# A transformer's four layers on one core: matmuls of constants put into TensorE's waits, and other banks for an MLP's first chunk

## The reference

```python
# first block, per layer; h_lat is (256, 1024), h_ctx is (256, 1024)
a_lat = modulate(rms_norm(h_lat, norm1_w[layer]), ml[0], ml[1])
o_lat, o_ctx = even_mixer(...)      # layer 0: latent attention and gated linear attention
o_lat, o_ctx = odd_mixer(...)       # layer 1: gated delta rule, 8 heads
h_lat = h_lat + ml[2] * o_lat
h_lat = h_lat + ml[5] * sq_relu_mlp(modulate(rms_norm(h_lat, norm2_w[layer]), ml[3], ml[4]), w1, w2)
# second block, per layer
h = rms_norm_2(x, mix_norm_pre[l]) * (1.0 + sc_m) + sh_m
y = hybrid_mixer(h, ...)            # top-k attention and a chunked mLSTM
x = x + g_m * rms_norm_2(y, mix_norm_post[l])
h = rms_norm_2(x, ffn_norm_pre[l]) * (1.0 + sc_f) + sh_f
y = swiglu(h, w_gate_up[l], w_down[l])
x = x + g_f * rms_norm_2(y, ffn_norm_post[l])
```

## Time and profile before

| | us |
|---|---|
| median of 3 executions | 2164.08 (2161.91 to 2165.92) |
| the profiled execution | 2163.82 |
| its span, first to last instruction | 2161.9 |
| TensorE busy in it | 2004.4 (93%) |
| VectorE busy | 1521.2 (70%) |
| ScalarE busy | 907.6 (42%) |
| mean granted clock of TensorE | 0.959 |

### The profile page before, as it was taken

One profiled execution on the slowest core, in us unless ns is written; L12 is line 12 of the kernel. 1 busy time (PEld: TensorE's weight loads), 2 busy tenths in 40 slices (PEclk: granted clock), 3 DMA queues, 4 the chain that ended last, 5 costly groups with the idle time before them and its releaser, 6 DMA issues. The chain is left out here.

```text
span 2161.9 us, 39923 instructions
## 1 busy us (share of the span) xinstructions
PE 2004.4 (93%) x16706; PEld 1788.0 (83%) x16706; DVE 1521.2 (70%) x2353; ACT 907.6 (42%) x1355; POOL 142.3 (7%) x231
## 2 busy tenths in 40 slices
PE   6998988999999889899999999799899979999997
PEld 5786765788888678798888999789789979988997
DVE  6866557798777668765647787689776667966454
ACT  2435453222222244423225444456544345554443
POOL 0100000001010001201210000000000000000000
PEclk7999989999999989999999999799999999999999
DMA  8542013356453176200004777343358744323552
GB/s 326 203 145 78 2 59 136 136 176 213 161 200 145 58 255 211 104 4 3 3 3 156 250 269 272 127 165 126 136 189 285 270 152 157 136 99 120 192 177 95
DMA packets 59132, 323.92 MB, mean 150 GB/s; under 512 B 6384, under 2 KB 7536, under 8 KB 32624
## 3 DMA queue, kind: packets, MB, share of 16 engines
q1 hardware_dynamic: 33360, 228.97, 29.7%
q0 software_dynamic: 25344, 92.29, 12.0%
q10 hardware_dynamic: 288, 0.66, 0.1%
HBM read 320.84 MB, written 1.05 MB: 149 GB/s over the span
## 5 line engine op out<-in xcount | busy, mean ns | idle before, releaser
L370 DVE TENSOR_TENSOR w_low<-raw,w_high 128x1024 fp32r<-128x1024 f32 (+1 forms) x408 | 473.4, 1202 | 196.9 <-ACT w_high L362 196.7
L362 ACT ACTIVATE w_high<-raw 128x1024 fp32r<-128x1024 f32 (+1 forms) x408 | 402.6, 1034 | 363.0 <-PE banks L407 352.3
L548 DVE SCALAR_TENSOR_TENSOR mod_rows<-mod_rows,silu_condition 128x1024 f32<-128x1024 f32 x176 | 212.9, 1221 | 9.0 <-DMA mod_rows<-rows_dram 6.3
L405 PE MATMUL banks<-ffn_a_l,w_high 128*128 128x256 f32 x704 | 201.1, 286 | 8.5 <-DVE ffn_a_l L712 6.5
L406 PE MATMUL banks<-ffn_a_h,w_high 128*128 128x256 f32 x704 | 199.3, 283 | 0.0
L407 PE MATMUL banks<-ffn_a_h,w_low 128*128 128x256 f32 x704 | 199.1, 283 | 0.0
L534 POOL DMA_DIRECT2D mod_rows<-rows_dram x176 | 93.2, 530 | 1329.7 <-DVE mod_rows L548 1108.6
L405 PE MATMUL banks<-mlp_hidden_l,w_high 128*128 128x512 f32 (+1 forms) x512 | 174.7, 341 | 3.9 <-DVE mlp_hidden_l L1102 3.0
L407 PE MATMUL banks<-mlp_hidden_h,w_low 128*128 128x512 f32 (+1 forms) x512 | 174.5, 341 | 0.0
L406 PE MATMUL banks<-mlp_hidden_h,w_high 128*128 128x512 f32 (+1 forms) x512 | 174.4, 341 | 0.0
L405 PE MATMUL banks<-mix_l,w_high 128*128 128x256 f32 (+1 forms) x448 | 134.4, 300 | 14.0 <-DVE mix_l L759 12.9
(11 more groups left out here) (617 smaller groups left out, 4983.3 us busy)
## 6 DMA issues: line engine op xcount, KB each, us to landing
raw<-panels_dram SPq DMA_DIRECT2D x204, 1024.0 KB, 4.8
mod_rows<-rows_dram POOLq DMA_DIRECT2D x176, 512.0 KB, 5.1
mod_0a_rows<-rows_dram SPq DMA_DIRECT2D x8, 1024.0 KB, 19.3
x_features<-x_features_dram SPq DMA_DIRECT2D x1, 2048.0 KB, 11.2
constants<-small_dram SPq DMA_DIRECT2D x1, 1672.5 KB, 6.7
silu_condition<-conditions_dram SPq DMA_DIRECT2D x2, 512.0 KB, 12.4
out_dram<-x_features SPq DMA_DIRECT2D x4, 256.0 KB, 2.1
constants<-small_dram SPq DMA_DIRECT2D x1, 736.5 KB, 5.1
```

What stands on the lines that cost most here:

```text
L362: self.nc.scalar.activation(self.wh[:, m % 2, cols], self.raw[:, slot, cols], ACT.Copy).then_inc(self.w_high, 1)
L370: self.nc.vector.tensor_tensor(self.wl[:, m % 2, cols], self.raw[:, slot, cols], self.wh[:, m % 2, cols].bitcast(F32), ALU.subtract).then_ ...
L405: self.nc.tensor.matmul(out, sh(k), ml(k), start=(opens and k == 0), stop=False)
L548: nc.vector.scalar_tensor_tensor(row if v == nv - 1 else self.scratch[:], row, 1.0, self.cond[v][:], ALU.mult, ALU.mult, accum_out=mod[:, ...
```

## The change

Two new methods issue float32 matmuls of the constant `ones` matrix with the first 512 columns of the constants, into a bank that is free, and nobody reads the result: `keep_busy` inside a TensorE function, and `busy_before` as a function of its own. `rstd` gets a parameter `busy = (first, last, bank)`: so many ahead of the sums of squares, and so many behind them. Calls stand ahead of `even_in`, `odd_in` and `mix_in`, in the attention ahead of turns 2, 8 and 30 and ahead of the last values, in the odd mixer ahead of the first keys and in the heads' norm, at the hybrid mixer's end, in the norms, and ahead of layer 1's MLP openers. `open_sums` uses all 128 rows instead of one. In layer 0's MLP the chunks from the second on take banks 2 and 3, and the second chunk's up products no longer wait for `h_ready`.

```diff
--- before.py
+++ after.py
@@ -559,7 +559,7 @@
     def rstd(self, tmp, name, src, src_ready, groups, n, dim, matrix, bank=0, squares=None,
-             meanwhile=None, r=None, between=None, fold=0, squared=None):
+             meanwhile=None, r=None, between=None, fold=0, squared=None, busy=None):
@@ -608,8 +608,11 @@
                 act.wait_ge(root_ready, 1)
                 nc.scalar.activation(r[:], root[:], ACT.Exp, scale=-0.5).then_inc(ready, 1)
+        busy_first, busy_last, busy_bank = busy or (0, 0, 0)
+
         @self.block.tensor
         def _(pe):
+            self.keep_busy(pe, busy_first, busy_bank)
             for i, blocks in enumerate(groups):
                 if fold:
                     blocks = [0] + blocks[fold:]
@@ -625,6 +628,7 @@
                     last = nc.tensor.matmul(sums[:, i, :], matrix, squares[:, b, :],
                                             start=(b == blocks[0]), stop=(b == blocks[-1]))
             last.then_inc(summed, 1)
+            self.keep_busy(pe, busy_last, busy_bank)
         @self.block.vector
         def _(dve):
@@ -635,10 +639,10 @@
                 nc.vector.reciprocal(r[:], root[:]).then_inc(ready, 1)
         return r, squares, [(ready, 1)]
-    def next_norm(self, scope, name, n, ready, split=False, squares=None):
+    def next_norm(self, scope, name, n, ready, split=False, squares=None, busy=None):
         return self.rstd(scope, name, self.xT[:, :, 0:n], ready, [list(range(KD))], n, D, self.c("ones"), 1, squares,
-                         r=self.next_rstd[:, :, 0:n],
+                         r=self.next_rstd[:, :, 0:n], busy=busy,
                          between=(lambda act: self.split_upto("act", act, self.m)) if split else None,
                          meanwhile=(lambda dve, _: self.split_upto("dve", dve, self.m)) if split else None)
@@ -663,7 +667,7 @@
         return [(ready, nb)]
     def norm_modulate(self, name, weight, mod, nv, shift, scale, n, high, low, ready, bank=0, work=None,
-                      scaled_x=None, split_first=2):
+                      scaled_x=None, split_first=2, busy=None):
         nc = self.nc
@@ -693,7 +697,7 @@
                     last.then_inc(scaled, 1)
             r, _, r_ready = self.rstd(tmp, name, x, ready, [list(range(KD))], n, D, self.c("ones"), bank, work,
-                                      meanwhile=scale_x)
+                                      meanwhile=scale_x, busy=busy)
             @self.block.vector
             def _(dve):
@@ -936,9 +940,18 @@
     def open_sums(self, pe, banks):
-        zero, any_rows = self.c("causal")[0:1, TL:TL + P], self.cst[0:1, 0:512]
+        zero, any_rows = self.c("causal")[:, TL:TL + P], self.cst[:, 0:512]
         for b in banks:
             self.nc.tensor.matmul(self.ps[:, b, :], zero, any_rows, start=True, stop=False)
+
+    def keep_busy(self, pe, count, bank):
+
+
+        for _ in range(count):
+            self.nc.tensor.matmul(self.ps[:, bank, :], self.c("ones"), self.cst[:, 0:512], start=True, stop=True)
+
+    def busy_before(self, count, bank):
+        self.block.tensor(lambda pe: self.keep_busy(pe, count, bank))
     def open_sums_first(self, banks=(5, 6, 7)):
         self.block.tensor(lambda pe: self.open_sums(pe, banks))
@@ -975,7 +988,7 @@
         ps = self.ps
         scaled_ready, bias_ready = (self.sem(f"{name}_{s}") for s in ("scaled", "shift_product_ready"))
         bias = self.sb(f"{name}_shift_product", [P, 2, 1], ctx=tmp)
-        first_bank = 2 if deferred is not None else 0
+        first_bank = 0 if gated else 2
         up_banks = lambda cs: slice(0, 2) if cs == 0 else slice(first_bank, first_bank + 2)
         def pe_up_deferred(pe, cs, q=None):
@@ -1028,12 +1041,12 @@
             for u in range(ups):
                 self.wait_split(pe, m_of["up", cs, u], q)
                 m = m_of["up", cs, u]
-                if u == 0 and cs >= 1:
+                if u == 0 and cs >= (1 if gated else 2):
                     pe.wait_ge(h_ready, c)
                 for b in range(2):
                     if cs == 0 and u == 0 and b == 0:
                         self.operand_wait = lambda k: pe.wait_ge(a_ready[0][0], k + 1)
-                    last = self.product3(ps[:, 2 * u + b, 0:n],
+                    last = self.product3(ps[:, 2 * u + b if gated else up_banks(cs).start + b, 0:n],
                                          lambda k: self.wh[:, m % 2, k * PC + b * P:k * PC + (b + 1) * P],
                                          lambda k: self.wl[:, m % 2, k * PC + b * P:k * PC + (b + 1) * P],
                                          lambda k: high[:, k, 0:n], lambda k: low[:, k, 0:n], KD)
@@ -1075,7 +1088,7 @@
             if cs >= 1:
                 act.wait_ge(h_ready, c)
             act.wait_ge(up_done, c * ups + 1)
-            nc.scalar.activation(act_buf[:], ps[:, 0:2, 0:n], ACT.Silu if gated else ACT.Relu).then_inc(r_ready, 1)
+            nc.scalar.activation(act_buf[:], ps[:, up_banks(cs), 0:n], ACT.Silu if gated else ACT.Relu).then_inc(r_ready, 1)
         def act_high(act, cs, q=None):
             c = cs if q is None else q * per + cs
@@ -1093,7 +1106,7 @@
             if gated:
                 ins = nc.vector.tensor_tensor(hid[:], act_buf[:], ps[:, 2:4, 0:n], ALU.mult)
             else:
-                ins = nc.vector.scalar_tensor_tensor(hid[:], ps[:, 0:2, 0:n], 0.0, act_buf[:], ALU.max, ALU.mult)
+                ins = nc.vector.scalar_tensor_tensor(hid[:], ps[:, up_banks(cs), 0:n], 0.0, act_buf[:], ALU.max, ALU.mult)
             ins.then_inc(h_ready, 1)
         def dve_low(dve, cs, q=None):
@@ -1601,6 +1614,7 @@
             nc.vector.tensor_tensor(flat(cq_l[:]), flat(pa[:, 0:3, :]), flat(cq_h[:]).bitcast(F32),
                                     ALU.subtract).then_inc(cq_split, 1)
+    pr.busy_before(4, 6)
     pr.linear("even_in", 7, 2, 14, pr.features(high, low, N, KD, tall_offset), pr.copy_out(target), a_ready,
               beside=beside_in, rising=True, info=in_info)
@@ -1748,10 +1762,13 @@
         scores(2)
         for n in range(T):
             if n + 1 < T:
+                pr.keep_busy(pe, {2: 4, 8: 1, 30: 3}.get(n + 1, 0), 2)
                 turn(n + 1)
             if n + 3 < T:
                 scores(n + 3)
             gla_step(n)
+            if n + 1 == T:
+                pr.keep_busy(pe, 2, 2)
             values(n)
         for n, i in enumerate((0, 2, 1, 3)):
             pe.wait_ge(a_scaled, n + 1)
@@ -2142,6 +2160,9 @@
                 nc.tensor.matmul(ps[:, b, :], c("block64"), kT[:, b, :], start=True, stop=True).then_inc(k_summed, 1)
         def turn_keys(h):
+            if h == 0:
+                pe.wait_ge(logs, 3)
+                pr.keep_busy(pe, 3, 3)
             pe.wait_ge(normed, h + 1)
             for b in (2 * h, 2 * h + 1):
                 for i in range(4):
@@ -2653,6 +2674,8 @@
     def _(pe):
         for d in range(2):
             for h in range(2):
+                if d and not h:
+                    pr.keep_busy(pe, 2, 2 * order[1])
                 pe.wait_ge(sq_ready, 2 * d + h + 1)
                 nc.tensor.matmul(ps[:, 2 * order[d] + h, :], c("ones"),
                                  sq[:, order[d], 4 * h:4 * h + 4, :].rearrange("p h n -> p (h n)"),
@@ -2842,6 +2865,7 @@
             eng.wait_ge(cq_high, 1)
             nc.vector.tensor_tensor(cq_l[:], cq_sq, cq_h[:].bitcast(F32), ALU.subtract).then_inc(cq_split, 1)
+    pr.busy_before(3, 7)
     pr.linear("mix_in", 4, 2, 8, pr.features(high, low, N, KD, tall_offset), block_out(0), a_ready,
               engines=who[:8], rising=True, beside=beside_first, info=a_info, first_out=conv_first(0))
     sm_t = work[0:32, 0, :]
@@ -3195,6 +3219,8 @@
                                            hm[:, i, b * P:(b + 1) * P], c("ident"))
             last.then_inc(m_turned, 1)
         for i in range(2):
+            if i:
+                pr.keep_busy(pe, 2, 1)
             pe.wait_ge(o_scaled, i + 1)
             for b in range(4):
                 last = nc.tensor.transpose(ps[:, (4, 5)[b // 2], (b % 2) * N + i * P:(b % 2) * N + (i + 1) * P],
@@ -3325,10 +3351,11 @@
                 high = pr.sb("mlp0_a_h", [P, KD, n], F32R, ctx=t)
                 low = pr.sb("mlp0_a_l", [P, KD, n], F32R, ctx=t)
                 a_ready = pr.norm_modulate("norm2_0", norm("norm2", 0), mod, nv, 24, 32, n, high, low,
-                                           lambda k: [(ready[0][0], k + 1)], bank=0, scaled_x=y)
+                                           lambda k: [(ready[0][0], k + 1)], bank=0, scaled_x=y,
+                                           busy=(2, 7, 1))
                 y, y_ready = pr.feed_forward("mlp0", D_FF // 256, False, n, high, low, a_ready, y, [], beside)
                 added = pr.add_feed_forward("mlp0", y, y_ready + outs[0], mod, 40, nv, n)
-                pr.next_norm(t, "norm1_1", n, lambda k: [(added[0][0], k + 1)], split=True)
```

(16 more changed lines are left out.)

## The result

| | us |
|---|---|
| median of the kernel before, 4 executions | 2163.49 (2161.91 to 2165.92) |
| median of the changed kernel, 4 executions | 2151.7 (2148.91 to 2156.08) |
| ratio | 0.9946, 95% interval 0.9933 to 0.9959 |
| the profiled execution of the changed kernel | 2156.08, the longest of its four; span 2154.3 |

The change makes the kernel 11.8 us faster (9 to 14.5 by the interval). I had forecast 16.6 us. The sign and the main mechanism were right; the size was 40% too large (two later measurements give 12.6 and 13.3 us, and at 13.3 it is a quarter too large).

The account below looks back on a forecast made before the run. TensorE was taken to set the time at half clock for microseconds after waits at hand-overs, with filler costing nothing. Terms of 15.05 us plus 1.5 for the banks gave 16.55 us, so 2147.5 us, range 2137 to 2160.

Parts of the forecast that it names:

- odd_in: Odd mixer's input products: some 13 after a_l is complete at 0.12 instead of 0.21 us each, 1.3 us gained.
- mix_in: First projections of each of two mixers: products at 0.12 instead of 0.21 us, taken as 0.7 and 1.0 us.
- norm2_0: A norm's 16 passes for the sums of squares: 8.83 us down to about 7.0 at full clock, 1.8 us gained.
- turn(8): In the attention: four transposes and two score passes at full clock while VectorE is idle, 1.2 us gained.
- even_out: Dip at 302 to 312 us: the first 24 products end at 313.4 instead of near 315.6, 2.2 us gained.
- mix_out: Two places with all operands there and the last ten products at full clock: 1.4 us each, 2.8 us together.
- The banks: First MLP: chunk 1 no longer waits for chunk 0's hidden values; 1.5 us gained, bounds 0 and 3.9.
- even_in and the other small ones: even_in, odd_out, odd keys and mix_pre_1, where operands or another engine set the pace: 1.6 us together, an estimate.
- The filler does not hold the clock: Rival: constants nobody reads may leave or move the dips; only the banks' 1.5 us stay, 2162.5 us, chance 0.08.
- Other engines keep the time: Rival: terms ending where VectorE is nearly full vanish, 8.5 us of the gain; 2156 us, chance 0.15.
- Slower: Rival: the changed kernel is slower than the one before, 2182 us, chance 0.06.
- more comes back: Rival: all dips gone, VectorE and ScalarE follow, banks give 3.9 us; 30 us gained, 2134 us, chance 0.10.

Follow-up runs that it names:

- the run of the norms' filler: Only the constant products of the norms put into the kernel before, nothing else of the change: 2158.39 us, ratio 0.9982.

## Why the prediction was right in sign and too high in size

**What bounds the kernel.** Right in the main. The gain sits at the hand-overs, and the same number of instructions with 127 rows fewer gives none of it (2163.25 us beside 2163.86). That a dip always begins in or behind a wait of 1.5 to 10 us is too strong, and so is that each lies at a hand-over: in the first profile of the kernel before, two lie inside the odd mixer behind waits of at most 0.96 us, and the first begins while TensorE is busy. Their windows, TensorE alone:

```profile
25.90:26.90 1.00, 1.00 (x7) 0.50 1.02 406
957.80:961.00 3.20, 2.90 (x56) 0.50 0.00 0
1015.80:1019.00 3.20, 3.20 (x66) 0.50 0.02 5
```

In every stretch shown here the granted clock is 0.50 or 1.00, or a mean of the two where it changes inside. By these two levels the mean clock of 0.959 makes 177 us at half clock over the span, 34 of them in the first 60. TensorE is busy in most of that time, 4.69 of 4.70 us in one row and 4.65 of 4.70 in another. By an estimate from the starts (spacing beside that of the same pair of products at full clock) the products in the dips lost some 70 us before and lose about 35 in the changed kernel, 13 of these in the first 60 us in both. So some 35 us less is lost, and 11 us came out at the end. The rest was followed by another wait. The time at half clock itself fell from 177 to 77 us (mean clock 0.982); half of that difference would be 50 us, four times what was measured, and it would come back only if TensorE set the time in every dip.

**The filler costs nothing.** Nearly right in total, wrong in three places. At layer 0's end all engines meet and TensorE pauses, 3.27 us here and 1.72 where two more fillers run ahead of it; the clock fell there (half from 752.8 to 756.2), and the four fillers ahead of odd_in then ran mostly at half clock, 5.37 instead of 3.4 us, and the first product came right behind them with no wait between, which was a sign that I had named for "wrong". At the first mix_in the last filler is likewise followed by the first product without a wait. It cost little, as VectorE's operands set the pace soon behind it. The filler ahead of even_in makes VectorE wait 1.2 us longer for a row at 105 us, in eight of nine profiles, and takes as much as it gives. Doubling shows how much room there is: 46 of 58 added us lie hidden. The prices were about right: the seven fillers behind norm2_0's sums took 6.17 us at full clock (forecast 6.0), and the four ahead of even_in, mostly at half clock, 5.61, 6.42 and 6.36 us in the three profiles (forecast 6.8).

**The terms.** norm2_0, norm1_1, mix_pre_0, turn(8), even_out, mix_in and the first mix_out came within 0.6 us of their values in this pair of profiles. For turn(8), norm2_0, norm1_1 and mix_pre_0 that holds in all three profiles of the changed kernel. For even_out it holds in two, and mix_in and mix_out were gained in part where they had no filler, so that these two came out right is partly luck. Three steps failed:

- *odd_in, 1.3 us, got +0.7.* The step that failed is my assumption under all the terms, that the filled waits hold the full clock in the stretch behind. No run shows that as a rule. Here the stretch behind is itself sparse: three short products for each operand, and 0.7 to 0.9 us of waiting ahead of four of the eight. The fillers ahead of it ended before this began, and the clock fell in the middle. The size was right: with a filler ahead of each operand 1.7 us came back.
- *The banks, 1.5 us, got 0.* I set the end of chunk 1's products at 404.0 and reached the sum banks 5.6 us behind that, later than the copy-out at 408.0. But 404.0 is the old end, with the wait and the dip in it. Without these 3.9 us the products end at about 400 and TensorE is at the sum banks at 404.8, 2.7 us ahead of VectorE. The wait that I had looked for in my list of signs ("about 2 us in its place") was the thing that took the whole gain, and a dip came with it. I had the lower bound, 0, and took the middle from a sum in which old and new times were mixed. (The 1.3 us of the first profile came because no dip followed the wait there; a stage without new banks gave the same in the run of the norms' filler.)
- *even_in and the other small ones, 1.6 us.* The small ones gave 1.5, but the stage up to even_in's end lost 2.0. VectorE waits longer for a modulation row there (2.61 beside 1.38 us), and TensorE waits at 141. This cost doesn't stand in my sum at all: I had set every transfer at nothing since none was added. Over the whole kernel VectorE's waits for rows are 20.6 us in the changed kernel and 13.5 in the kernel before (second profiles).

A second loss of this kind, which comes and goes with the execution, can be read in layer 1's projections. From the first profile of the kernel before, VectorE and then TensorE:

```profile
794.20 1.22 DVE L548 SCALAR_TENSOR_TENSOR mod_rows<-mod_rows,silu_condition 128x1024 f32<-128x1024 f32 x1 [0.96 <-DMA mod_rows<-rows_dram]
...
798.54 0.47 PE L405 MATMUL banks<-a_l,w_high 128*128 128x512 f32 x1 [0.77 <-ACT odd_conv L1913]
```

And from the first profile of the changed kernel:

```profile
794.14 1.23 DVE L548 SCALAR_TENSOR_TENSOR mod_rows<-mod_rows,silu_condition 128x1024 f32<-128x1024 f32 x1 [3.82 <-DMA mod_rows<-rows_dram]
...
798.04 0.67 PE L405 MATMUL banks<-a_l,w_high 128*128 128x512 f32 x1 [3.19 <-DVE w_low L370]
```

The row lands at the same time; VectorE comes to it 2.9 us earlier and waits that much longer. The split of the next weights is queued behind it, so TensorE waits 3.19 us for `w_low`. Its products start 0.5 us before those of the kernel before, with a wait that is 2.4 us longer. TensorE's waits for `w_low` went from 5.7 us to 10.0, 8.7 and 6.7 in the three profiles of after, which is the way to miss that the prediction named last, only by rows and not by mix_in's own gain. How often a row is late changes from one execution to the next: the three profiles of the changed kernel have 20.9, 20.6 and 14.5 us of such waits, at spans of 2154.3, 2149.9 and 2149.1. Little of the shortfall in the median can be put down to the rows in this stage, as the third profile has almost none of it (0.2 us) and is only 0.8 us shorter than the second. No run here says what delays the transfers.

**The sum, again,** against the table of steps: 16.55 forecast; less 1.5 and 0.3 for the banks, 2.0 for odd_in, 3.2 for the two stages with late rows, 0.1 for the small ones, 1.4 for the second mix_out (which gave its 1.5 in the other pair of profiles); plus 1.3 at mlp1's end and the final norm, which I had set to nothing, and 1.45 by which turn(8), even_out and mix_in, less the norms' small shortfalls, gave more than I took. That is 10.8 us, beside 10.9 between these two profiles and 11.8 and 12.6 between the medians. So 8.5 us that I had too much met 2.75 that I had too little, and it was luck that these took a part of the miss away.

**The rivals.** "The filler does not hold the clock" fell with the measured ratio, and one-row fillers show the very kernel it described, at 2163.25 us (forecast for it 2162.5). "Other engines keep the time" is right in two of its five terms, odd_in and the banks, and wrong in turn(8), mix_in and mix_out. "Slower" did not happen, not even with twice the filler (2163.26 us beside 2164.73), and no run shows its 2182 us. Nor did "more comes back" (2134): with five more places filled it is 2145 us.

## What to carry to other kernels

Read the granted clock beside the waits of TensorE: if it falls behind a wait and TensorE then sets the time, products of constants with all their rows in that wait cost little and gave 0.5% here, and 0.9% with five more places, among them the gaps between slowly arriving operands. Price such a place by the products that are dense and on the path behind the wait, not by the time at half clock, and count the filler so that it ends before the wait does: twice as much took the whole gain away (2163.26 us). Don't put a step down to its own filler from one profile: dips come and go with what was filled ahead of them. When a wait is removed, work out the new times of everything behind it before asking who is late next.

## What the runs showed of the chip that I had not expected

- TensorE's clock did not follow occupation in time here. One-row passes that kept it busy for 7.48 us let it fall to 0.50; 128-row passes by a matrix of zeros held it at a mean of 0.984, as ones did (0.982). From 25.8 to 47.5 us in the second profile of the changed kernel TensorE is busy without a break (21.70 of 21.70 us) with products of 128 rows by two columns (`mod_0a_rows`, L486 in the profile) and is granted 0.50 of the clock all that time; the kernel before shows the same (21.70 of 21.70 us, 0.50). So full rows alone did not hold it either.
- The clock fell in the middle of odd_in behind waits of 0.7 to 0.9 us ahead of three operands, although no single one was long, and in the kernel with twice the filler behind two of 0.8 and 0.9 us.
- The same unfilled wait of 2.46 us in mlp0 was followed by half the clock in both profiles of the kernel before and by full clock in the run of the norms' filler.
- VectorE's waits for the modulation rows (512 KB each) vary between 13.5 and 22.3 us from one profile to the next although all kernels make the same transfers, and between 14.5 and 20.9 us for the changed kernel alone.
